# Depthwise convolution of a decoder trunk moved from VectorE taps to banded products on TensorE

## The reference

```
h = rmsnorm(x) @ w_in                     # 1024 -> 3140 columns
u = ua * sigmoid(ub)                      # 512 channels
y[t, c] = sum_k u_ext[t + k, c] * conv_w[k, c] + conv_b[c]     # causal, 31 taps
yn = (y - mean_c(y)) * rsqrt(var_c(y) + 1e-5) * ln_g + ln_b    # over the 512 channels
conv = silu(yn) * silu(gc)
```

## Time and profile before

| | us |
|---|---|
| median of three runs | 1948.4 |
| profiled execution | 1948.56 |
| its span, first to last instruction | 1946.9 |
| PE busy | 1531.3 (79%) |
| DVE busy | 1366.8 (70%) |
| ACT busy | 737.0 (38%) |
| POOL busy | 407.8 (21%) |

### The profile page before, as it was taken

One profiled execution on the slowest core, in us unless ns is written; L12 is line 12 of the kernel. 1 busy time (PEld: TensorE's weight loads), 2 busy tenths in 40 slices (PEclk: granted clock), 3 DMA queues, 4 the chain that ended last, 5 costly groups with the idle time before them and its releaser, 6 DMA issues. The chain is left out here.

```text
span 1946.9 us, 26700 instructions
## 1 busy us (share of the span) xinstructions
PE 1531.3 (79%) x9511; PEld 1287.0 (66%) x9511; DVE 1366.8 (70%) x2361; ACT 737.0 (38%) x1271; POOL 407.8 (21%) x297
## 2 busy tenths in 40 slices
PE   6879959699659939792768888888888767369998
PEld 5876959689649939792456666665665545247776
DVE  3413988688879888886259998988789997134442
ACT  3525411332142232231214554555445444344441
POOL 2120314234204303431300100001000111232211
PEclk9989979899879969896768998999899997579999
DMA  7632452113256402321511110110102111613333
GB/s 243 211 73 47 95 95 69 66 52 91 65 199 139 101 21 74 93 59 42 159 56 47 41 54 1 54 54 29 52 28 76 37 49 61 203 65 129 120 125 108
DMA packets 166186, 164.59 MB, mean 85 GB/s; under 512 B 54666, under 2 KB 137618, under 8 KB 166047
## 3 DMA queue, kind: packets, MB, share of 16 engines
q1 hardware_dynamic: 165031, 160.80, 27.9%
q0 software_dynamic: 1024, 2.10, 0.3%
HBM read 100.94 MB, written 57.93 MB: 82 GB/s over the span
## 5 line engine op out<-in xcount | busy, mean ns | idle before, releaser
L674 PE MATMUL psum<-xh,wh 128*128 128x384 f32 (+1 forms) x1056 | 348.1, 330 | 34.0 <-POOL wl L550 32.5
L1256 DVE SCALAR_TENSOR_TENSOR cy<-cu,cw,cy 128x1088 f32<-128x1088 f32 x240 | 350.3, 1460 | 15.8 <-issue 0.7
L674 PE MATMUL psum<-xh,wl 128*128 128x384 f32 (+1 forms) x1056 | 347.1, 329 | 0.0
L674 PE MATMUL psum<-xl,wh 128*128 128x384 f32 (+1 forms) x1056 | 347.1, 329 | 0.0
L1159 ACT ACTIVATE pts<-psT 128x512 f32<-128x512 f32 (+1 forms) x302 | 168.5, 573 | 314.9 <-PE psT L1426 292.3
L674 PEld LDWEIGHTS psum<-xh,wh 128*128 128x128 f32 x1056 | 200.3, 190 | 35.8 <-issue 21.4
L1418 PE MATMUL psU<-kh,qt 128*128 128x512 f32 (+3 forms) x320 | 138.5, 434 | 92.2 <-DVE mx L1310 90.9
L1442 PE MATMUL psO<-pts,vs 128*64 128x128 f32 x2176 | 185.2, 292 | 23.6 <-ACT pts L1159 23.4
L674 PEld LDWEIGHTS psum<-xl,wh 128*128 128x128 f32 x1056 | 200.5, 190 | 0.0
L674 PEld LDWEIGHTS psum<-xh,wl 128*128 128x128 f32 x1056 | 200.2, 190 | 0.0
L1426 PE MATMUL psT<-cst,L 128*128 128x128 f32 x1105 | 184.8, 300 | 11.0 <-ACT L L1187 10.7
(11 more groups left out here) (270 smaller groups left out, 2535.1 us busy)
## 6 DMA issues: line engine op xcount, KB each, us to landing
wst<-in_w_in SPq DMA_DIRECT2D x28, 512.0 KB
wst<-in_w_in SPq DMA_DIRECT2D x32, 256.0 KB
qt<-d_q SPq DMA_DIRECT2D x16, 512.0 KB, 4.1
xst<-in_x_prompt SPq DMA_DIRECT2D x15, 512.0 KB, 3.9
xr<-in_x_prompt SPq DMA_DIRECT2D x15, 512.0 KB, 4.4
out_y_prompt<-fin SPq DMA_DIRECT2D x15, 512.0 KB, 2.9
gate<-d_ga SPq DMA_DIRECT2D x17, 256.0 KB, 4.4
d_mix<-mix SPq DMA_DIRECT2D x17, 256.0 KB, 2.1
```

Source lines behind the costliest of these rows:

```text
L674: last = nc.tensor.matmul(u[:, 0:k * P], a[:, w % 2, cc, :], x[:, s0:s0 + k, cc, :], start=(cc == 0 and e == 0), stop=(cc == KC - 1 and e ...
L1256: V.scalar_tensor_tensor(y, u[:, k:k + HALFW], w, y, ALU.mult, ALU.add)
```

## The change

**Second stage.** After each block of `ua` a job `uT` transposes the product `u` back to token by channel on TensorE, one proj job later; ScalarE copies it, and SP writes it to `d_un`, in groups of 64 channels: partition is the token within its tile. `ust` takes the place of `lst` instead of a buffer of its own. SP first writes zeros ahead of `d_un`, and the conv weights into `d_cw` with 33 rows of zeros before and 32 behind.

**Third stage.** The 248 taps go. Tokens are cut in windows of 32: 65 for the prompt and 8 for the samples. For a channel, 64 rows of weights by 32 columns hold the 31 taps as a band (`ht`, one DMA in which each row starts 64 numbers later than the last), and the moving operand is one column for each window with its 32 rows and the 32 before it (`uw`). Four channels lie in a set, at rows 0 or 64 and at output columns 0, 32, 64, 96. There are 20 jobs of up to 7 such sets, one to two a step in steps 2 to 16, each after the products of its step. VectorE adds the bias as it empties PSUM into `yc`. `ht` and `uw` hold a quarter of the channels and are loaded again for the next quarter. From step 18 on the tiles are normalised two at a time in `yc`: sums over a partition's 128 channels on VectorE, over the four partitions of a token by one small matmul, then squares (GpSimd), again sums, a power (GpSimd) and a product (VectorE). Five steps after its sums a pair is turned by TensorE (4 matmuls a tile), copied by ScalarE and written to `d_y`.

**Fourth stage.** Only stage c is left. The channels now stand in another order over the partitions, so that `gc`, the first four pieces of `w_out` and the gains and offsets come in four DMAs each where there was one. The last rows of `u` go from `d_un` to the outputs by DMA.

```diff
 def select_jobs():
...
-            jobs += [("proj", h, c, b) for b in range(len(blocks))]
+            for b in range(len(blocks)):
+                jobs.append(("proj", h, c, b))
+                put_late()
+                if name == "ua":
+                    late.append(("uT", h, j, b))
...
+                elif job[0] == "uT":
+                    m = stage_of_u[job[1:]]
+                    pe.wait_ge(combined, m + 1)
+                    for e in range(slots(job[1], job[3])[1]):
+                        last = nc.tensor.transpose(u[:, e * P:(e + 1) * P], ust[:, m % 2, e * P:(e + 1) * P], ident)
...
+NQ, QA = 4, 32
+BANKA = 512 // NW
+CONV_JOBS = [(q, a, min(BANKA, QA - a)) for q in range(NQ) for a in range(0, QA, BANKA)]
+CONV_STEPS = [(2, 3, 3, 4, 4), (6, 7, 7, 8, 8), (10, 11, 11, 12, 12), (14, 15, 15, 16, 16)]
+NORM = [[LAST]] + [[i - 1, i] for i in range(LAST - 1, 0, -2)]
+SUM_STEP = [18 + 4 * k for k in range(len(NORM))]
+SQ_STEP = [s + 3 for s in SUM_STEP]
+TURN_STEP = [s + 5 for s in SUM_STEP]
...
+            def load_windows(q):
+                if q:
+                    sp.wait_ge(pe_pt, last_conv(q - 1))
...
+                for r in range(2):
...
+                    sp.dma_start(ht[a0:a2, :, :].rearrange("p m c -> p (m c)"),
+                                 bass.AP(t.d_cw.tensor, b * HROWS * CB, [[CB, WROWS], [1, WIN * CB]])).then_inc(ht_in, 16)
+                    sp.dma_start(uw[a1:a2, 0:main, :].rearrange("p (w i) c -> p w (i c)", w=WPT),
+                                 u[:, CB:(LAST + 1) * CB].rearrange("(w p) x -> p w x", p=WIN)).then_inc(uw_in, 16)
...
-            def conv_tap(tap):
...
-                    V.scalar_tensor_tensor(y, u[:, k:k + HALFW], w, y, ALU.mult, ALU.add)
...
+            def convolved(e, q, a, k):
...
+                TT(yc[:, :, c].rearrange("p n a -> p a n"), pt[:, 0:k * NW].rearrange("p (a n) -> p a n", n=NW),
+                   cbt[:, c].unsqueeze(2).to_broadcast([128, k, NW]), ALU.add).then_inc(conv_out, 1)
...
+            def convolve(e, q, a, k):
+                pt = take_pt(("C", e))
...
+                for x in range(k):
+                    for g in range(4):
+                        r, c = g // 2, QA * (g % 2) + a + x
+                        last = T.matmul(pt[WIN * g:WIN * g + WIN, x * NW:(x + 1) * NW], ht[64 * r:64 * r + WROWS, :, c],
+                                        uw[64 * r:64 * r + WROWS, :, c], start=True, stop=True,
+                                        tile_position=(64 * r, WIN * g))
+                last.then_inc(pe_pt, 1)
...
+            def turn(k, i):
+                pt = take_pt(("Y", k, i))
...
+                    for w in range(WPT):
+                        last = T.matmul(pt[:, w * P:(w + 1) * P], yc[:, w * LAST + i, :], flip[:, 0, :], start=True, stop=True)
...
+        schedule = [("c", 0), ("tile", LAST), ("c", 1)]
...
+                if e == 1 and k + 1 < NB:
+                    schedule.append(("c", k + 1))
...
-                if w_next < KC:
+                while w_next < KC and (k == 0 or w_next < KC - 2):
                     w_high(w_next)
```

More of the change, by code:

```diff
@@ L90, in constants @@
     at("ones")[:] = 1.0 / C
+    for r in range(128):
+        at("flip")[r, r // WIN * WIN + WIN - 1 - r % WIN] = 1
+        at("avg")[r, r % WIN::WIN] = 1.0 / C
     return c
@@ L372, in select_jobs, with put_late @@
 def select_jobs():
-    jobs = []
+    jobs, late = [], []
+    def put_late():
+        jobs.extend(late)
+        late.clear()
     for h, blocks in enumerate(HALVES):
@@ L535, in _ @@
             sp.wait_ge(r_out, 16)
+            for s in range(2):
+                sp.wait_ge(ut_out[s], 16 * len(ut_jobs[s::2]))
             for k in range(3):
@@ L923, in attend_and_convolve @@
     NP_ = len(pairs)
-    ujobs = [("kT", g, n) for g in range(len(KEYS)) for n in range(NKV)] + [("cw", 0), ("S", 0)]
+    ujobs = [("kT", g, n) for g in range(len(KEYS)) for n in range(NKV)] + [("S", 0)]
     for p, (i, j) in enumerate(pairs):
@@ L941, in attend_and_convolve @@
     band0 = lambda i: max(0, (i - 1) * P)
[L943 to L949, removed]
     LW = NT * P
@@ L1323, in _ @@
                     finish(tile_no[pairs[p - 2][0]])
-                for tap in range(dtaps[p], dtaps[p + 1]):
-                    conv_tap(tap)
+                for e, (q, a, k) in enumerate(CONV_JOBS):
+                    if CONV_STEP[e] == p - 1:
+                        convolved(e, q, a, k)
+                for k in range(len(NORM)):
+                    if TURN_STEP[k] == p:
+                        normalise(k)
+                    if SQ_STEP[k] == p:
+                        square_sums(k)
+                    if SUM_STEP[k] + 2 == p:
+                        subtract_mean(k)
+                    if SUM_STEP[k] == p:
+                        sums(k)
                 if p == 0:
@@ L1348, in take_pt @@
                 if n >= 2:
-                    pe.wait_ge(act_pt, n - 1)
+                    back = ptjobs[n - 2]
+                    if back[0] == "C":
+                        pe.wait_ge(conv_out, back[1] + 1)
+                    else:
+                        pe.wait_ge(act_pt, act_copies(back))
                 return PT[:, n % 2]
@@ L1361, in _ @@
             pe.wait_ge(c_in, 32)
-            pe.wait_ge(cw_in, 16)
-            u = take_u(("cw", 0))
-            for c in range(CC):
-                last = T.transpose(u[:, c * TAPS:(c + 1) * TAPS], cwn[:, c * P:(c + 1) * P], ident[0:TAPS, 0:TAPS])
-            last.then_inc(pe_u, 1)
             pe.wait_ge(s_in, 64)
@@ L1606, in _ @@
                 if c < CC:
-                    sp.dma_start(wst[:, c % WS, :], t.w_out[0, c * P:(c + 1) * P, :]).then_inc(w_ld[c % WS], 32)
+                    for q in range(NQ):
+                        r = P * q + QA * c
+                        sp.dma_start(wst[QA * q:QA * q + QA, c % WS, :], t.w_out[0, r:r + QA, :]).then_inc(w_ld[c % WS], 16)
                 else:
@@ L1835, in _ @@
                     n += 1
-                    continue
-                w = len(BLOCKS[k]) * P
-                if what == "a":
-                    pe.wait_ge(y_in[k % 2], 32 * (k // 2 + 1))
-                    if k == 0:
-                        pe.wait_ge(ys_done, 1)
-                    else:
-                        pe.wait_ge(centred, k)
-                    for c in range(CC):
-                        last = T.matmul(ST[:, 0, 0:w], ones, y[:, k % 2, c, 0:w], start=(c == 0), stop=(c == CC - 1))
-                    last.then_inc(mean_done, 1)
-                elif what == "b":
-                    pe.wait_ge(squared, k + 1)
-                    if k:
-                        pe.wait_ge(std_done, k)
-                    for c in range(CC):
-                        last = T.matmul(ST[:, 1, 0:w], ones, tmp[:, c, 0:w], start=(c == 0), stop=(c == CC - 1))
-                    last.then_inc(var_done, 1)
 class Tensors:
```

459 lines of the change are left out of this document (270 added, 189 removed).

## The result

The changed kernel takes 1896.6 us (median of 4, 1895.2 to 1898.7) against 1949.2 (4 runs, 1946.8 to 1954.7): ratio 0.973, 95% interval 0.970 to 0.975, -52.6 us. Forecast were 1913 and a range of 1883 to 1963.

The account below looks back on a forecast made before the run. VectorE was taken to bound the second stage, VectorE and TensorE nearly full in the third, TensorE the fourth. 1948.6 + 1 (second) - 5 (third) - 32 (fourth) = 1912.6, so 1913 us; own range 1895 to 1930, with rivals up to 1963.

Parts of the forecast that it names:

- (a): Third stage, first step: seven taps between the sample products and the scaling go, so TensorE's logits wait less; -10 us.
- (b): Third stage: TensorE's 81.0 us of waits for VectorE at the logits shrink to 32 us; -49, ends -33 and -59.
- (c): Third stage: of the 8.9 us TensorE waits before reciprocals that stood behind taps, -6 us, ends 0 and -8.9.
- (d): Third stage: with less TensorE idling the granted clock spends less time at 1.2 GHz; -12 us, ends 0 and -37.
- (e): Third stage: convolution matmuls on TensorE, 1024 records at 31.4 ns plus job starts, all on the path; +38 us.
- (f): Third stage: turning the normalised tiles by full matmuls on TensorE, copies hidden on ScalarE; +19 us, ends 12 and 30.
- (g): Third stage: eighteen single-matmul sums on TensorE at some 0.35 us each; +6 us.
- (h): Third stage: normalisation chains on VectorE and GpSimd fit, but hold up logits in tiles 2 to 5; +4, ends 0 and 12.
- (i): Third stage: window loads of 3.2 MB a quarter need 28 us, wanted after 26 to 32; +5 us, ends 0 and 30.
- Rival 1: Third-stage convolution: the array's quarters don't run side by side, 61 ns a record, +30 us, 1943 us; chance 0.16.
- rival 3: Third-stage convolution: strided reading at half pace with two quarters side by side, 63 ns, +32 us, 1945 us; chance 0.08.
- Rival 2: Third stage: more is won, clock stays up (-20 more), windows and chains cost nothing (-9); 1884 us; chance 0.12.

Follow-up runs that it names:

- b_no_taps: The kernel before with 240 of its 248 convolution taps left out, loads and writes kept; 1845.3 us, ratio 0.944.

## Why the prediction was right, and where it was not

Of the 50 us between the two traces 36 were forecast. The third stage came out 29 us better than forecast and the other three together 15 us worse, so part of the closeness is errors that cancel.

The third stage by the prediction's terms, in us. The shares of TensorE's time are summed from start to next start over the timeline, the waits taken from the list of its waits.

| step | forecast | measured |
|---|---|---|
| (a) first step | -10 | -11.1 |
| (b) logit waits | -49 | -52.0 |
| (c) reciprocals | -6 | -8.9 |
| (d) clock | -12 | -33 (the rest) |
| (e) convolution | +38 | +37.5 |
| (f) turning | +19 | +19.2 |
| (g) small sums | +6 | +4.4 |
| (h) chains of the normalisation | +4 | +9.8 |
| (i) windows | +5 | 0 |

- **(d) is the step that failed.** "Idle time is shortened, not abolished, so I take -12, ends 0 and -37": the mechanism was right, the size was off by 21 us, and with it the third stage is 29 us below the forecast, beyond the 15 us that were set as a test. The time at 1.2 GHz fell by some 93 of 118 us. By the prediction's own working (three quarters of it work, half of that back) 93 us are worth 35, near the 33 of the table. So what failed is the share of this time that goes: I took a third (12 of 37), and it was about four fifths, although waits of up to 1.6 us stay. That the taps did it is shown by b_no_taps (0.94 for 0.88 over the stage, and some 30 us beyond the waits, in the durations of the same matmuls). That a faster clock gives them without the slack is not: filling the waits gave 9. The 33 are a rest, with the small changes of the waits for ScalarE in it.
- **(e) is right by luck: two errors cancel.** I took 31.4 ns from a form in which two halves take turns and operands lie side by side. The array runs four quarters side by side (15.0), and the stride costs 2.1 (31.7). Rival 1 failed in its premise, rival 3 was true in its own (half pace) but not in its price, since its base was twice too high. The 32 ns "floor of load and issue" doesn't exist.
- (b) hung on the estimate of what the steps keep, and that was near: 29.0 us against 32. (h) was too low: VectorE comes 6.5 us late at worst before the turning matmuls. (i) no wait on a window load shows. The evacuations take 0.99 us, not 0.7, beside TensorE's work.
- **Second stage.** "The idle time there is at least 12.2 us, so VectorE still sets the end": the view was of the last four groups only. Ahead of them VectorE waits 9.6 us for ScalarE, and what is added on TensorE there counts in full.
- **Fourth stage.** From the first product on the stage is 28.5 us shorter, against some 27 by the forecast (the 26, and the second tile 1.5 us closer behind the first). "4 to 8 us" for the small DMAs was 16: I priced their issue and not their rate, so that the start is 4.7 us later and not 5 earlier.
- Rival 2 (1884) named two things that came, the clock and windows that cost nothing. Its third, chains that cost nothing, did not (9.8 us), and that it gives 1897 with the second and the fourth stage at their measured lengths is in part luck: (b) and (c) gave 6 us more than both it and the forecast said.

## What to carry to other kernels

What an edit on a side engine is worth is decided by the slack of the step: here half of the work removed gave 93% of the gain, so ask first how much must go. Give matmuls that share the array a moving operand that lies side by side (worth 20 us here; a kernel that lays its windows out so and computes the convolution wasn't run), and count how many quarters really run together before taking a pace from another form. A load cut to fit a layout should be priced by its rate and by the number of engines it is spread over, and not by its issue alone.

## What the runs showed of the hardware that I had not expected

- Matmuls of 64 rows x 32 columns in four column quarters, two of each row half, into one PSUM bank, run four at a time: 15.0 ns a record against 62 where all lie in one quarter of one row half.
- 256 bytes between the elements of the moving operand cost a factor of 2.1 (31.7 ns a record against 15.0); between those of the weights nothing that shows.
- While DMAs with 4 as the outermost dimension on the DRAM side ran, the engines moved mostly 100 GB/s; with four DMAs to 32 partitions each mostly 160 to 220; with one to 128 partitions 230 to 430. Other loads ran beside them in all three.
